# Samples' tile first in the first combine, and the Toeplitz copies of a block issued half by SyncE and half by ScalarE

## The chip, the cores and the metric

The program runs on one core of a Trainium2 chip. The metric is the device time of one launch in microseconds. The engines are TensorE (PE, with PEld for its weight loads), VectorE (DVE), ScalarE (ACT), GpSimd (POOL) and SyncE (SP). SP and ACT also issue DMAs, in program order among their other instructions; a row with SPq or ACTq is such an issue. All data is fp32.

## What is computed

One inference step of a two-layer decoder trunk for 512 prompt tokens and 8 x 8 sample tokens, 576 tokens of width 1024. Layer 0 mixes tokens by sliding-window attention, layer 1 by a diagonal complex state-space layer (S5). After each mixer a mixture of 32 experts with two experts per token is added. Cut to what matters here:

```python
for layer in range(2):
    x += mixer(rmsnorm(x))            # layer 0: attention, layer 1: S5
    x += hier_moe(rmsnorm(x))         # 32 experts, top 2, softmax weights
y = rmsnorm(x)                        # the final norm

# S5: 64 channel groups of 16, each driving a 64-dim complex diagonal state
u = xn.reshape(seq, 64, 16)
bu = einsum('lgc,gpc->lgp', u, bbar)  # complex
h = associative_scan(a_bar, bu)       # over positions
y = real(einsum('lgp,gcp->lgc', h, c)) + d * u
z = gelu(y)
out = (z @ w_a) * sigmoid(z @ w_b)    # the GLU
```

## The kernel before

**Tiles of tokens.** The 576 tokens lie in five tiles of `X`: tiles 0 to 3 are the prompt, 128 tokens each, and tile 4 holds the 64 sample tokens. `XN` holds their normed rows.

**End of the first expert layer.** Sixteen pairs of experts run in order. GpSimd gathers the tokens of a pair and scatters the pair's output rows to `y_scratch` in HBM. SP issues the weight loads (L453 and L459), then the load of a table (L495), the state of the samples (L498), and, once all rows are stored, `rows_back`: five reads of `y_scratch` (L486), tile 0 first. VectorE adds the two rows of each token to `X` (L1476, two instructions a tile, the "combine") and norms the tile before (L737, L740); ScalarE makes the sum of squares and the root between them (L714, L717). Behind `rows_back` SP issues the loads of the first four "blocks" (L376 with `block_scratch`, 1472 KB each), and behind these it waits for each normed tile and copies it from SBUF to SBUF into another layout `AL` (L507), which puts the eight positions of a chunk side by side in one partition: 72 chunks, 64 of the prompt and 8 of the samples. The copy of a prompt tile writes 16 partitions, that of the samples' tile 8.

**The S5 blocks.** The state-space layer runs over `NB` = 8 blocks of 8 channel groups, pipelined by hand: a loop over k on every engine, in which block k enters and block k-2 leaves.

- GpSimd copies the channels of block k out of `AL` (L694, `u_gather`; the first waits for all five copies).
- TensorE: `scan_inputs` transposes the block's weights (L1901) and its inputs (L1909), `taps` makes the taps of a short convolution (L1937), `chunk_sums` the sums of the chunks (L1921), `outputs` the results of block k-2 (L1951, L1955), `mixed_transposed` transposes the results of block k-3 (L1966). L1909 and L1966 write the same PSUM banks, so L1909 of block k waits until the results of block k-4 are copied out.
- ScalarE, in this order in iteration k: copies out the transposed weights (L992) and inputs (L997, L999), GELU of block k-2 (L1005), a copy of the start states (L1009), the taps into `KP` (L1015, four instructions), from k = 2 on the load of block k+2 (L1021), and the transposed results of block k-3 (L1025, two instructions; PE's L1909 waits for them).
- VectorE adds the skip weights to the taps (L1509, which signals `taps_ready`), turns and scans the chunk sums (L1511 to L1528).
- SP waits for `taps_ready` and issues eight copies of 64 KB, SBUF to SBUF (L514), which lay the taps out as a Toeplitz matrix `TT`: one copy for each of the eight shifts, 16 partitions each. `outputs` waits for all eight.

Behind the blocks come the GLU (L2005), the second expert layer and the final norm.

**What sets the order.** Each engine runs the order that is written out in the code; nothing is planned at run time. DMAs issued by SP share one queue, those issued by ACT another. `keep_busy(n, b)` (L1553) is a run of matmuls whose result nobody reads.

## Time and profile before

| what | us |
|---|---|
| median of 3 runs | 944.31 (942.0 to 945.46) |
| profiled execution, its own time | 951.33 |
| span of the profiled execution | 949.6 |
| PE busy | 771.1 (81%) |
| DVE busy | 406.6 (43%) |
| ACT busy | 260.1 (27%) |
| POOL busy | 151.9 (16%) |

Times in the views are microseconds from the start of the span. In a row of the chain of waits the first number is the start, the second the time, and behind them stands what held the chain: an engine with tile and line, a DMA, or an engine's queue. In a row of the timeline the same two numbers are followed by engine, line, operation, output and inputs, and, in brackets, how long the engine had been idle and what ended that. Averages over the span hide the stages: from 482 to 528 PE is nearly idle, and the chain of waits runs through DVE and a DMA there.

### The profile page before, as it was taken

Reading aid. Unit: us, or ns where it says so; the run is one execution under the profiler, and the core shown is the slowest. Engines: PE = TensorE matmul, PEld = TensorE weight load, DVE = VectorE, ACT = ScalarE, POOL = GpSimd, SP = SyncE. Lnnn points to the kernel's source line nnn. Section 1 sums busy time; section 2 is a strip of 40 time slices with the busy share of each in tenths; the row PEclk is TensorE's granted clock in tenths of the full one; section 3 lists DMA queues with packets and bytes.
Section 4 is the critical chain, followed back from the end, with each engine's and each line's share of the span. In section 5 each row is a group of like instructions: output and inputs, shape, how many; then the busy total and the mean of one; then the engine's idle time right before and its main releaser. Section 6 shows DMA issues by size and latency. Waiting matters only on the chain.

```text
span 949.6 us, 12702 instructions
## 1 busy us (share of the span) xinstructions
PE 771.1 (81%) x4843; PEld 480.9 (51%) x4843; DVE 406.6 (43%) x1001; ACT 260.1 (27%) x554; POOL 151.9 (16%) x233
## 2 busy tenths in 40 slices
PE   4999977998999889996810579899999989997840
PEld 3444446777545775554500457644345487554520
DVE  3478686766678441211145556500112162121118
ACT  6020035534121102321131345320014312232113
POOL 1010003000978012332000201000000002322110
PEclk9999996969999789999965789999999979999785
DMA  9461153000633988999779368690041194999946
GB/s 344 135 212 75 50 180 144 2 1 4 212 138 118 335 335 310 409 411 407 304 260 323 46 169 196 136 385 1 17 161 45 68 396 162 408 409 410 402 149 233
DMA packets 74806, 201.81 MB, mean 213 GB/s; under 512 B 14809, under 2 KB 29529, under 8 KB 73689
## 3 DMA queue, kind: packets, MB, share of 16 engines
q1 hardware_dynamic: 57784, 161.77, 47.2%
q0 software_dynamic: 9696, 19.75, 6.0%
q10 hardware_dynamic: 7264, 19.46, 5.6%
q8 instruction: 40, 0.66, 0.3%
q14 instruction: 22, 0.17, 0.1%
HBM read 171.64 MB, written 39.39 MB: 222 GB/s over the span
## 4 chain that ended last, share of the span: by engine, by line
PE 57%; DMA 14%; DVE 11%; SPq 7%; ACT 6%; issue 3%; POOL 0%; PEldq 0%; DVEq 0%; POOLq 0%; PEld 0%; ACTq 0%
PE PSUM L2005 13%; PE PSUM L1598 8%; PE PSUM L1813 8%; PE PSUM L1757 7%; SPq L453 4%; DMA XNT<-in_moe_w_up 4%; PE PSUM L1833 3%; DMA RING<-in_attn_w_qkv 3%; DMA PH<-in_moe_w_up 2%; DVE X L1476 2%; PE PSUM L1801 2%; DMA RING<-XNT 2%; PE PSUM L1688 2%; PE PSUM L1955 2%; PE PSUM L1951 2%
## 5 line engine op out<-in xcount | busy, mean ns | idle before, releaser
L1598 PE MATMUL PSUM<-RING,XNT 128*128 128x512 f32 (+2 forms) x256 | 94.3, 567 | 3.0 <-DMA RING<-in_attn_w_qkv 2.3
L638 POOL DMA_INDIRECT PH<-xn_scratch,PH x32 | 32.6, 1020 | 354.3 <-DVEq L1421 245.6
L2005 PE MATMUL PSUM<-PH,XNT 128*128 128x512 f32 (+1 forms) x220 | 88.1, 593 | 0.3 <-PE PSUM L2005 0.3
L1813 PE MATMUL PSUM<-RING,PH 128*64 128x256 f32 x384 | 75.8, 412 | 13.1 <-DMA PH<-in_moe_w_up 6.6
L1813 PE MATMUL PSUM<-PH 128*64 128x256 f32 x384 | 68.6, 412 | 8.7 <-DMA RING<-in_moe_w_up 5.9
L1452 DVE TENSOR_TENSOR PH<-PH,PSUM 128x128 f32<-128x128 f32 x32 | 9.3, 289 | 145.8 <-ACT PH L943 145.8
L1598 PEld LDWEIGHTS PSUM<-RING,XNT 128*128 128x128 f32 (+1 forms) x256 | 40.3, 177 | 52.4 <-issue 47.7
L1757 PE MATMUL PSUM<-RING,PH 128*128 128x512 f32 (+1 forms) x160 | 62.6, 593 | 0.0
L1813 PEld LDWEIGHTS PSUM<-RING,PH 128*64 128x64 f32 x384 | 44.7, 149 | 34.3 <-issue 18.8
L2005 PEld LDWEIGHTS PSUM<-PH,XNT 128*128 128x128 f32 (+1 forms) x220 | 36.3, 179 | 47.6 <-issue 47.5
L1537 DVE TENSOR_TENSOR PH<-PSUM,PH 128x512 f32<-128x512 f32 (+1 forms) x10 | 6.9, 691 | 115.4 <-ACT PH L1047 115.4
L1813 PEld LDWEIGHTS PSUM<-PH 128*64 128x64 f32 x384 | 40.5, 149 | 28.2 <-issue 13.1
L714 ACT ACTIVATE XNT<-X 128x1024 f32<-128x1024 f32 (+1 forms) x25 | 26.4, 1054 | 103.1 <-DVE X L1334 52.9
L938 ACT ACTIVATE PH<-PSUM 128x1024 f32<-128x1024 f32 x32 | 32.8, 1026 | 67.6 <-PE PSUM L1801 67.6
L647 POOL DMA_INDIRECT y_scratch<-PH x32 | 32.0, 1002 | 91.2 <-DVE PH L1447 89.8
L2005 PE MATMUL PSUM<-RING,XNT 128*128 128x512 f32 (+1 forms) x100 | 43.2, 610 | 1.3 <-ACT XNT L1025 1.3
L1447 DVE COPY PH<-PSUM 128x512 f32<-128x512 f32 x32 | 22.2, 692 | 49.6 <-PE PSUM L1833 25.8
L1757 PEld LDWEIGHTS PSUM<-RING,PH 128*128 128x128 f32 (+1 forms) x160 | 26.3, 179 | 33.2 <-issue 33.2
L943 ACT ACTIVATE PH<-PSUM 128x128 f32<-128x128 f32 x32 | 8.9, 278 | 123.8 <-PE PSUM L1813 123.8
L1555 PE MATMUL PSUM<-ONES,IDENT 128*128 128x128 f32 x296 | 41.0, 308 | 0.2
L1555 PEld LDWEIGHTS PSUM<-ONES,IDENT 128*128 128x128 f32 x296 | 40.3, 223 | 0.5 <-PEq L312 0.5
L1801 PE MATMUL PSUM<-IDENT,PH 128*128 128x128 f32 x256 | 37.4, 290 | 2.2 <-DMA PH<-xn_scratch,PH 2.2
(378 smaller groups left out, 1387.9 us busy)
## 6 DMA issues: line engine op xcount, KB each, us to landing
RING<-in_moe_w_gate SPq DMA_DIRECT2D x24, 512.0 KB
RING<-in_moe_w_up SPq DMA_DIRECT2D x24, 512.0 KB
PH<-in_moe_w_gate SPq DMA_DIRECT2D x24, 512.0 KB
PH<-in_moe_w_up SPq DMA_DIRECT2D x24, 512.0 KB
RING<-in_moe_w_down SPq DMA_DIRECT2D x24, 512.0 KB
PH<-in_moe_w_down SPq DMA_DIRECT2D x24, 512.0 KB
XNT<-in_moe_w_gate SPq DMA_DIRECT2D x16, 512.0 KB
XNT<-in_moe_w_up SPq DMA_DIRECT2D x16, 512.0 KB
```

Of the source, the lines that this page charges most:

```text
L453: sp.dma_start(r[:, w * D:(w + 1) * D].rearrange("p (c f) -> p c f", c=KC), src[layer, e].rearrange("(p c) f -> p c f", p=P)).then_inc(S(f ...
L638: pool.indirect_dma_start(out=XG[:, i % 2, :], out_offset=None, in_=xn_d[layer], in_offset=bass.IndirectOffsetOnAxis(ap=IDX[:, i:i + 1], a ...
L647: pool.indirect_dma_start(out=y_d[layer], out_offset=bass.IndirectOffsetOnAxis(ap=IDXS[:, i:i + 1], axis=0), in_=YB[:, i % 2, :], in_offse ...
L714: nc.scalar.activation(XN[0:r, t, :], X[0:r, t, :], ACT.Square, accum_out=SS[0:r, n, t:t + 1]).then_inc(S("squares"), 1)
L938: nc.scalar.activation(XGT[:, i % 2, :, :], bank(0, 2).rearrange("p b (c t) -> p (b c) t", c=4), ACT.Copy).then_inc(S("xgt_ready"), 1)
L1555: te.matmul(PSUM[:, b, 0:P], IDENT[:, :], ONES[:, :], start=True, stop=True)
L1598: last = te.matmul(PSUM[lo:hi, b0 + col // 512, col % 512:col % 512 + n], XT[:, c, t * P:t * P + r], RING[:, c // 2, (c % 2) * QKV + col:( ...
L1757: last = te.matmul(PSUM[p0:p0 + r, 4 + 2 * (t % 2) + n, :], OT[:, c, t * P:t * P + r], slot(SLOT[q])[:, (c % 3) * D + n * 512:(c % 3) * D ...
L1801: last = te.transpose(PSUM[:, c // 4, (c % 4) * P:(c % 4 + 1) * P], xg[:, c, :], IDENT[:, :])
L1813: last = te.matmul(PSUM[m * 64:(m + 1) * 64, 2 + i % 2, 0:2 * FF], XGT[:, i % 2, c, m * 64:(m + 1) * 64], gu[:, :, c, :], start=(c == 0), ...
L1833: last = te.matmul(PSUM[m * 64:(m + 1) * 64, 4 + 2 * b + n, :], HID[:, b, m, :], r[:, 2 * D + n * 512:2 * D + (n + 1) * 512], start=True, ...
L2005: last = te.matmul(PSUM[p0:p0 + r, 2 * (i % 2) + w, :], XT[:, c, t * P:t * P + r], slot(SLOT[q])[:, (2 * (c % 3) + w) * 512:(2 * (c % 3) + ...
```

## The change

Six edits, all between the end of the first expert layer and the end of the S5 blocks:

1. `rows_back(0)`, the combine and the norm of that place go over the tiles in the order 4, 0, 1, 2, 3 (`TILES`, `tiles`, `place`); so do the copies into `AL`.
2. The loads of blocks 0 and 1 are issued by SP right behind the last expert weights; those of blocks 2 and 3 behind the copies into `AL`.
3. SP issues the first four of the eight Toeplitz copies of a block, ACT the other four, behind its taps (L1015) and ahead of its copy of the transposed results (L1025).
4. ACT issues the load of block 4 in iteration 3 behind L999, not at the end of iteration 2. Blocks 5 to 7 stay where they were.
5. PE runs 16 matmuls of `keep_busy` when all five tiles are combined, ahead of the barrier that ends the stage.
6. PE runs 10 more behind the transposed weights of block 0.

```diff
+        TILES = {2: (4, 0, 1, 2, 3)}
...
             def rows_back(layer):
                 sp.wait_ge(S("all_stored"), layer + 1)
-                for t in range(NT):
+                for t in tiles(2 + 2 * layer):
...
             experts(0)
+            for k in (0, 1):
+                block_in(k)
             sp.wait_ge(S("ring_free"), Q_M0 + 28)
...
             rows_back(0)
-            for k in range(4):
-                ring_load(Q_SSM + k, [(slot(SLOT[Q_SSM + k])[:, 0:BLK_F], blk_d[k])])
-            for t in range(NT):
-                sp.wait_ge(S("xn_done"), 2 * NT + t + 1)
+            for t in tiles(2):
+                sp.wait_ge(S("xn_done"), place(2, t) + 1)
                 rows = AL[t:PCH:4, :, :] if t < 4 else AL[PCH:NCH, :, :]
                 sp.dma_start(rows, XN[0:ROWS[t], t, :]).then_inc(S("al_in"), 16)
+            for k in (2, 3):
+                block_in(k)
...
-                for sh in range(L):
+                for sh in range(L // 2):
                     sp.dma_start(TT[...], KP[...]).then_inc(S(f"toeplitz{k % 3}"), 16)
...
+                    if k == 3:
+                        block_in(4)
...
                     ins.then_inc(S("kp_ready"), 1)
-                    if 4 <= k + 2 < NB:
+                    if 5 <= k + 2 < NB:
+                        block_in(k + 2)
+                if k < NB:
+                    act.wait_ge(S("taps_ready"), k + 1)
+                    if k >= 3:
+                        act.wait_ge(S("y_ssm"), k - 2)
+                    for sh in range(L // 2, L):
+                        act.dma_start(TT[...], KP[...]).then_inc(S(f"toeplitz{k % 3}"), 16)
...
                     last.then_inc(S("st_transposed"), 1)
+                    pe.wait_ge(S("x_updated"), 2 * NT)
+                    keep_busy(16, 7)
                 end_phase(pe, ph)
...
                 last.then_inc(S("w_transposed"), 1)
+                if k == 0:
+                    keep_busy(10, 7)
```

On SP, between the last expert weights and the Toeplitz copies of block 1. Before (`in_moe_w_down` are the last expert weights, `input_scratch` the table, `RING<-XNT` the copies into `AL`, `PH<-PH` the Toeplitz copies), with the empty overflow branch between the states and `y_scratch` left out:

```order
L459 DMA XNT<-in_moe_w_down 128x1024 [waits expert_out] x2
L495 DMA PH<-input_scratch 128x1600 [waits ring_free]
...
L486 DMA XNT<-y_scratch 128x2x1024 x2
L486 DMA PH<-y_scratch 64x2x1024
L376 DMA RING<-block_scratch 128x2944 [waits ring_free]
L376 DMA PH<-block_scratch 128x2944 [waits ring_free] x3
L507 DMA RING<-XNT 16x8x1024 [waits xn_done] x4
L507 DMA RING<-XNT 8x8x1024 [waits xn_done]
L514 DMA PH<-PH 16x8x128 [waits taps_ready]
L514 DMA PH<-PH 16x8x128 x7
```

On SP, the same stretch in the changed kernel:

```order
L468 DMA XNT<-in_moe_w_down 128x1024 [waits expert_out] x2
L385 DMA RING<-block_scratch 128x2944 [waits ring_free]
L385 DMA PH<-block_scratch 128x2944 [waits ring_free]
L509 DMA PH<-input_scratch 128x1600 [waits ring_free]
...
L495 DMA PH<-y_scratch 64x2x1024 [waits all_stored]
L495 DMA PH<-y_scratch 128x2x1024 x2
L495 DMA XNT<-y_scratch 128x2x1024 x2
L519 DMA RING<-XNT 8x8x1024 [waits xn_done]
L519 DMA RING<-XNT 16x8x1024 [waits xn_done] x4
L385 DMA PH<-block_scratch 128x2944 [waits ring_free] x2
L528 DMA PH<-PH 16x8x128 [waits taps_ready]
L528 DMA PH<-PH 16x8x128 x3
```

No block load stands between the reads of `y_scratch` and the copies into `AL` any more; two went ahead of the reads and two behind the copies, and four of the Toeplitz copies left the queue.

On ACT, iteration 4 of the block loop, from GELU to the transposed weights of the next iteration. Before (`RING<-PSUM` is GELU, `PH<-XNT` the start states, `PH<-PSUM 16x2x128` the taps, `XNT<-PSUM` the transposed results, `RING<-PSUM 128x1024` the weights):

```order
L1005 ACTIVATE RING<-PSUM 72x4x8x16 [waits u_gathered,y_ssm]
L1005 ACTIVATE RING<-PSUM 72x4x8x16
L1009 ACTIVATE PH<-XNT 128x8x8
L1015 ACTIVATE PH<-PSUM 16x2x128 [waits toeplitz2,taps]
L1015 ACTIVATE PH<-PSUM 16x2x128 x3
L1021 DMA PH<-block_scratch 128x2944 [waits ring_free]
L1025 ACTIVATE XNT<-PSUM 128x8x64 [waits z_transposed]
L1025 ACTIVATE XNT<-PSUM 128x8x8
L992 ACTIVATE RING<-PSUM 128x1024 [waits g_done,w_transposed]
```

On ACT, the same iteration in the changed kernel:

```order
L1026 ACTIVATE RING<-PSUM 72x4x8x16 [waits u_gathered,y_ssm]
L1026 ACTIVATE RING<-PSUM 72x4x8x16
L1030 ACTIVATE PH<-XNT 128x8x8
L1036 ACTIVATE PH<-PSUM 16x2x128 [waits toeplitz2,taps]
L1036 ACTIVATE PH<-PSUM 16x2x128 x3
L1004 DMA PH<-block_scratch 128x2944 [waits ring_free]
L1046 DMA PH<-PH 16x8x128 [waits y_ssm,taps_ready]
L1046 DMA PH<-PH 16x8x128 x3
L1052 ACTIVATE XNT<-PSUM 128x8x64 [waits z_transposed]
L1052 ACTIVATE XNT<-PSUM 128x8x8
L1011 ACTIVATE RING<-PSUM 128x1024 [waits g_done,w_transposed]
```

A wait on VectorE's `taps_ready` and four DMA issues now stand between the taps and the copy of the transposed results.

## Rows read from the trace of the kernel before

**Rows 1.** Page, part 4: shares of the chain that ended last, by engine.

```profile
PE 57%; DMA 14%; DVE 11%; SPq 7%; ACT 6%; issue 3%; POOL 0%; PEldq 0%; DVEq 0%; POOLq 0%; PEld 0%; ACTq 0%
```

**Rows 2.** Chain of waits from the rows' return to the first block: start, time, what.

```profile
482.27 5.25 DMA PH<-y_scratch
...
507.11 1.29 DVE XNT L740
508.41 19.49 DMA RING<-XNT
...
528.02 1.04 POOL PH L694
```

**Rows 3.** Timeline of SP's issues in the same stretch: block loads, copies into AL.

```profile
485.86 1.41 SPq L376 DMA_DIRECT2D PH<-block_scratch  x3
494.55 14.60 SPq L507 DMA_DIRECT2D RING<-XNT  x5
```

**Rows 4.** Windows: span, busy PE, PEld, DVE, ACT, POOL, clock, DMA share, GB/s.

```profile
460.00:485.00 25.00, 15.29 (x114) 8.86 (x114) 3.24 (x7) 4.46 (x7) 3.92 (x4) 0.94 0.56 203
485.00:512.00 27.00, 1.97 (x8) 1.57 (x8) 22.75 (x27) 9.52 (x17) 0.00 (x0) 0.50 1.02 385
512.00:522.00 10.00, 0.00 (x0) 0.00 (x0) 1.86 (x5) 0.00 (x0) 0.00 (x0) 0.50 1.01 200
522.00:526.00 4.00, 0.00 (x0) 0.00 (x0) 0.00 (x0) 0.00 (x0) 0.00 (x0) 0.50 0.50 83
535.00:540.00 5.00, 3.38 (x80) 2.93 (x80) 4.86 (x9) 3.58 (x9) 1.59 (x2) 1.00 0.70 88
```

**Rows 5.** DMA issues by tile, with KB each and median us to landing.

```profile
out<-XNT SPq DMA_DIRECT2D x4, 512.0 KB, 2.6
```

**Rows 6.** Chain of waits, one period of the block loop (iteration 6).

```profile
582.06 0.59 ACT RING L1005
...
584.38 1.25 ACT XNT L1025 x2
...
585.77 0.69 PE PSUM L1909 x8
...
590.44 0.61 PE PSUM L1955 x8
```

**Rows 7.** Timeline of DVE: the taps' addition in iteration 5, and what it waited for.

```profile
574.95 0.29 DVE L1509 TENSOR_TENSOR PH<-PH 16x128 f32<-16x128 f32 x1 [2.02 <-ACT PH L1015]
```

**Rows 8.** Source views, ns min/median/max of one issue: Toeplitz copies on SP, ACT's issues.

```profile
L514 SPq DMA_DIRECT2D PH<-PH x64: 585/601/1811, 533.4 to 608.3; - x64
L1037 ACTq DMA_DIRECT2D out<-PH x4: 442/449/454, 623.3 to 625.2; - x4
L873 ACTq DMA_DIRECT2D out<-PH x1: 1038/1038/1038, 132.3 to 132.3; - x1
```

**Rows 9.** Timeline of PE: the outputs of blocks 1 and 7 begin.

```profile
555.57 1.13 PE L1951 MATMUL PSUM<-PH,XNT 128*72 128x128 f32 x4 [5.06 <-DMA PH<-PH]
...
611.65 1.13 PE L1951 MATMUL PSUM<-PH,XNT 128*72 128x128 f32 x4 [3.16 <-DMA PH<-PH]
```

**Rows 10.** Chain of waits: the outputs of blocks 1, 5 and 7 end.

```profile
561.91 0.61 PE PSUM L1955 x8
...
599.93 0.61 PE PSUM L1955 x8
...
617.32 0.61 PE PSUM L1955 x8
```

**Rows 11.** Windows before and after the outputs of block 7 begin, columns as in rows 4.

```profile
608.50:611.60 3.10, 0.00 (x0) 0.00 (x0) 1.10 (x4) 1.24 (x3) 0.00 (x0) 1.00 0.80 114
611.70:614.50 2.80, 2.80 (x16) 2.17 (x16) 0.00 (x0) 0.00 (x0) 0.00 (x0) 0.50 1.01 351
```

**Rows 12.** Timeline: keep_busy of 20 matmuls ahead of the experts, ACT's table load for GELU.

```profile
324.42 6.56 PE L1555 MATMUL PSUM<-ONES,IDENT 128*128 128x128 f32 x40
...
540.75 1.28 ACT L1005 ACT_TABLE_LOAD   x1
```

More of the change, by code:

```diff
@@ L359, in router_load, with tiles, place @@
             queue.dma_start(BR[:, 4:36], b_re_r[layer:layer + 1, :].to_broadcast([P, 32])).then_inc(S("router_in"), 16)
+        TILES = {2: (4, 0, 1, 2, 3)}
+        def tiles(n):
+            return TILES.get(n, range(NT))
+        def place(n, t):
+            return NT * n + list(tiles(n)).index(t)
         block = ctx.enter_context(nc.Block())
@@ L492, in _, with block_in @@
             sp.dma_start(in_d[:, 2 * GP * CH:], PWRQ.rearrange("p r k g -> p (r k g)")).then_inc(S("bb_out"), 16)
+            def block_in(k):
+                ring_load(Q_SSM + k, [(slot(SLOT[Q_SSM + k])[:, 0:BLK_F], blk_d[k])])
             experts(0)
+            for k in (0, 1):
+                block_in(k)
             sp.wait_ge(S("ring_free"), Q_M0 + 28)
@@ L711, in norm_act @@
             else:
-                act.wait_ge(S("x_updated"), NT * (n - 1) + t + 1)
+                act.wait_ge(S("x_updated"), place(n, t) - NT + 1)
             r = ROWS[t]
@@ L734, in norm_dve @@
         def norm_dve(dve, ch, n, t):
-            dve.wait_ge(S("roots"), NT * n + t + 1)
+            dve.wait_ge(S("roots"), place(n, t) + 1)
             r = ROWS[t]
             ch(nc.vector.reciprocal(RSTD[0:r, n, t:t + 1], RSTD[0:r, n, t:t + 1]))
-            if t == 0:
+            if t == tiles(n)[0]:
                 dve.wait_ge(S("gamma_in"), 16 * (n + 1))
@@ L980, in moe @@
                                          ).then_inc(S("hs_in"), 1)
-                for t in range(NT):
+                for t in tiles(2 + 2 * layer):
                     norm_act(act, 2 + 2 * layer, t)
@@ L985, in _, with block_in @@
             moe(0, 4)
+            def block_in(k):
+                q = Q_SSM + k
+                act.wait_ge(S("ring_free"), freed(q))
+                act.dma_start(slot(SLOT[q])[:, 0:BLK_F], blk_d[k]).then_inc(S(f"ring_full{SLOT[q]}"), 16)
             for k in range(NB + 3):
@@ L1017, in _ @@
                     ins.then_inc(S("kp_ready"), 1)
-                    if 4 <= k + 2 < NB:
-                        q = Q_SSM + k + 2
-                        act.wait_ge(S("ring_free"), freed(q))
-                        act.dma_start(slot(SLOT[q])[:, 0:BLK_F], blk_d[k + 2]).then_inc(S(f"ring_full{SLOT[q]}"), 16)
+                    if 5 <= k + 2 < NB:
[5 more added lines that the diff above has]
+                    for sh in range(L // 2, L):
+                        act.dma_start(TT[CH * sh:CH * sh + CH, k % 3].rearrange("p w g n -> p (w g) n"),
+                                      KP[k % 2][:, :, :, 112 - CH * sh:240 - CH * sh].rearrange("p w g n -> p (w g) n")
+                                      ).then_inc(S(f"toeplitz{k % 3}"), 16)
                 if k >= 3:
@@ L1470, in moe @@
                                            ).then_inc(S("ov_dve"), 1)
-                for t in range(NT):
+                norm = 2 + 2 * layer
+                for j, t in enumerate(tiles(norm)):
                     r = ROWS[t]
@@ L1477, in moe @@
                                                 in1=X[0:r, t, :], op0=ALU.mult, op1=ALU.add).then_inc(S("yg_used"), 1)
-                        dve.wait_ge(S("yg_used"), (layer * NT + t) * 2 + k + 1)
+                        dve.wait_ge(S("yg_used"), (layer * NT + j) * 2 + k + 1)
                     dve.sem_inc(S("x_updated"), 1)
-                    if t:
-                        norm_dve(dve, ch, 2 + 2 * layer, t - 1)
-                norm_dve(dve, ch, 2 + 2 * layer, NT - 1)
+                    if j:
+                        norm_dve(dve, ch, norm, tiles(norm)[j - 1])
+                norm_dve(dve, ch, norm, tiles(norm)[-1])
                 end_phase(dve, ph)
```

2 lines of the change are left out of this document (1 added, 1 removed).

## The prediction

> **What bounds the kernel now.** I read the page first, then the chain of waits. The chain is 57% PE and 14% DMA [rows 1], but the change touches only the stretch from the last experts to the GLU, so the page's shares decide nothing; that stretch has to be read by itself. There the chain runs through three things, and the reader should see them one after the other.
>
> First, the return of the rows: the read of tile 0 lands 5.25 us after its issue, at 487.5, VectorE then combines and norms five tiles until 508.4, and the last copy into `AL` lands 19.49 us later, at 527.9, when GpSimd begins block 0 [rows 2]. The windows say why that copy takes so long: the DMA engines are full at 385 GB/s from 485 to 512, then full at only 200 GB/s until 522, then half busy at 83 GB/s until 526 [rows 4]. The first stretch is the reads and the four block loads, 6.0 MB, which SP issued by 487.3, ahead of the first copy at 494.6 [rows 3]; the second is the copies, which queue behind them.
>
> Second, the loop over the blocks. From iteration 3 on it has a period of 9.5 us, one closed ring: GELU at 582.06, the other ACT work up to the transposed results at 584.38, PE's L1909 at 585.77, outputs until 591.05, GELU again [rows 6]. VectorE and SP hang on it with time to spare.
>
> Third, two waits of PE for Toeplitz copies, 5.06 us ahead of the outputs of block 1 and 3.16 us ahead of those of block 7 [rows 9].
>
> **The change part by part.** Sums are made against the profiled execution's own 951.33 us, which stands 7.0 us above the median of the runs; a difference is carried over as it is.
>
> *The return of the rows.* The samples' read is 512 KB, not 1024 KB, and is issued first. At the 385 GB/s of rows 4 half of 1 MB is 1.4 us; I take 1.2. The combine's chain of 20.9 us (487.5 to 508.4) has the same instructions, so it ends at 507.2. The last copy is now that of tile 3, 512 KB, with a queue that holds no block load ahead of it: the copies are 2.4 MB and at 200 GB/s one takes 2.6 us, under the 4.1 us that a tile takes on VectorE, so nothing piles up. A lone 512 KB store lands 2.6 us after its issue [rows 5], of which 1.3 are its bytes at 385 GB/s; 1.3 + 2.6 is 3.9 us, and with a tail as from 522 to 526 it would be 8. I take 4.4. So `AL` is complete at 511.6 instead of 527.9: **-16.3 us** (bounds -12.7 and -16.8).
>
> By the Trainium skill ("DMA: Bandwidth & Descriptors", "Why a DMA increments its semaphore by 16 and not by 1") a copy whose slower side has 8 partitions runs on 8 of the 16 engines, which would explain the half busy tail as the samples' copy; going first it would leave the end, and the term is -16.3. If the tail belonged to any such copy, the term would be -12.7; the rows alone don't tell the two apart.
>
> *Blocks 0 and 1 earlier.* 3.0 MB, 7.8 us at 385 GB/s. They are issued at about 458 behind the last weights, and from 460 to 485 the DMA engines are 44% idle [rows 4], 11 us. So they fit, at no cost; without that cover they would push the reads of `y_scratch` back by up to their own 7.8 us. Blocks 2 and 3 are issued behind the copies, at about 508, and land by 520, when the first Toeplitz copies are issued; block 2 is needed at about 522. No cost.
>
> *keep_busy.* 20 matmuls took 6.56 us from a cold start [rows 12], so 16 take some 5 us. They begin when the last tile is combined, at about 504, and end at 509, 1 us past VectorE; but GpSimd now waits until 511.6. VectorE's 5.4 us of set-up begin 1 us later and are needed at 517. The 10 further ones fit before 512.7. No cost; the first block starts warm, worth up to 1 us, which I leave out.
>
> *The start of the loop.* Split between two queues, with no block load beside them (block 4 is now issued later, past the copies of block 1), the Toeplitz copies of block 1 no longer hold PE: 5.06 us of wait and 2.3 us of slow clock behind it (6.95 us for those outputs [rows 9, 10] against 4.7 in rows 6) go away. Against that, ACT waits in iteration 1 until VectorE is done with block 0 and issues its four copies there; its 1.28 us table load, which lay in idle time [rows 12], comes out ahead of GELU. **-6.1 us.**
>
> *The period.* In iterations 3 to 7 ACT waits for `taps_ready` before it copies out the transposed results, and PE's L1909 waits for these; whatever ACT does there lengthens the ring. VectorE is already waiting for the taps [rows 7], so the wait is its 0.29 us and two signals, 0.4 us. The issues are not in the trace of before on ACT: their nearest row is the same copy on SP, 0.60 us [rows 8], 0.64 from one start to the next, 2.56 for four. ACT's other issues run from 0.45 to 1.04 [rows 8]; 0.60 is the same transfer, so I take it. 2.95 us more per period; between the outputs of block 1 and those of block 5 lie four periods (562.5 to 600.5 now [rows 10]): **+11.8 us** (bounds +8.8 and +18.2).
>
> *The clock.* PE reaches L1909 about when ACT is done now (ACT ends at 585.63, L1909 begins at 585.77 [rows 6]), so the 2.95 us become idle time of PE, once in each period. Ahead of the outputs of block 7 it idled 3.16 us, and came back at the lower of the clock's two levels, 1.2 GHz: granted clock 0.50 for 2.8 us [rows 9, 11]. Half speed for 2.8 to 3 us loses 1.4 to 1.5 us, in each of four periods: **+6.0 us** (bounds 0 and +9, the upper from the 4.5 us that the outputs of block 1 stayed slow).
>
> *The end of the loop.* From the outputs of block 5 to the end of those of block 7 it is 17.4 us now [rows 10]. Eight issues on SP are 5.1 us and the last lands 3.35 later; with four on each queue the issues take 2.6 us, and then the bytes bind: 512 KB at 88 GB/s and a share of 0.70 [rows 4] are 4.2 us of full DMA. So the copies land some 2 us earlier, PE's wait falls under 1.5 us, and with it 1.4 us of slow clock: **-3.1 us**.
>
> The Trainium skill ("DMA: Bandwidth & Descriptors", "Issuing engines are not separate DMA queues") speaks against the split: both queues feed the same 16 engines, and only the issue time is saved. By that alone this term would be -2.6, and by the rows -3.1.
>
> The sum: -16.3 - 6.1 + 11.8 + 6.0 - 3.1 = -7.7 us. Behind the loop (GLU, second experts) everything starts from the loop's end, so it moves along: 951.3 becomes 943.6 in a profile, and the median 944.3 becomes **936.6 us**.
>
> **The rivals.**
> - *A cheap ring.* PE's clock holds through the idle stretches, or ACT issues in 0.45 us as it does its small stores [rows 8], so that the idle stretch is 2.2 us. For it: 2.95 us is less than the 3.16 of rows 9. Against: by little. Without the 6.0 us of slow clock it gives -13.7; with 0.45 us an issue, 3 us less in four periods, -10.7 with the slow clock and -16.7 without: 927 to 934.
> - *A dear ring.* The clock stays down 4.5 us as it did from 555.5, or two queues slow each other's issues to 0.8 us. Then -1 to -4.5: 940 to 943.
> - *Slower than before.* ACT's issue of a copy costs what its store at L873 cost, 1.04 us. The period grows by 4.6 us, four times, with the slow clock behind it: 18.4 + 9 against 25.5 of gains and some 0.7 for the table load and iteration 2: +2 to +5, 946 to 949. With the slow clock at its upper bound it decides from 0.93 us an issue. Against it: L873 was issued right behind another store; no copy of the Toeplitz shape took over 0.6 us in the median.
> - *Not what it says.* Blocks 0 and 1 delay the last scatters or the reads, since the idle 44% is uneven between the 16 engines. The reads start 3 to 5 us later and the gain falls to 3 to 5 us: 939 to 941.
>
> **How the numbers follow.** The forecast 0.46; the cheap ring 0.26; the dear ring 0.15; late reads 0.07; slower 0.06. The range 927 to 943.5 leaves out the slow rival and the far ends of the cheap and the dear ring. A measurement of this kernel can tell about 0.5%, 4.7 us. Faster by more is the forecast, the cheap ring and a little of the late reads, 0.74; within it lie the rest of these, the dear ring and the near end of the slow rival, 0.22; slower, its far end, 0.04.
>
> **What would show each step.** The last copy into `AL` lands at about 512 and takes under 5 us. No DMA wait of PE ahead of the outputs of block 1. In iterations 4 to 7 four DMA issues on ACT between the taps and the transposed results, a period of 12.4 us with a granted clock of 1.00 or about 14 with 0.50 behind the idle stretch. The forecast is wrong if the copy still ends after 516, if the period stays at 9.5, or if it passes 15.

## The result, and the profile after

The changed kernel takes 964.28 us in the median (962.1 to 969.93), the kernel before 944.29 us (942.0 to 945.46) on the same chip: a ratio of 1.023, interval 1.019 to 1.027. It is slower by 20 us, where 936.6 was forecast, a gain of 8. The two profiled executions differ by less, 949.6 and 960.3 us of span: the one of before lay 7 us above its median, that of after 2 us below its own, and the code ahead of the changed stretch, the same in both, happened to take 5 us less in the latter.

Cut at five events that both traces have, the stretch reads as follows (each event's start, taken from the timelines of GpSimd and ACT; the GELU events are ACT's first GELU of a block).

| stage | before, us | after, us | difference | forecast |
|---|---|---|---|---|
| scatter of pair 12 to the issue of the reads of `y_scratch` | 21.6 | 26.9 | +5.4 | 0 |
| issue of the reads to GpSimd's first copy of block 0 | 45.8 | 32.1 | -13.7 | -16.3 |
| that copy to the GELU of block 1 | 34.5 | 30.5 | -4.0 | -6.1 |
| GELU of block 1 to GELU of block 5 | 38.0 | 66.4 | +28.4 | +17.8 |
| GELU of block 5 to GELU of block 7 | 17.4 | 17.5 | +0.1 | -3.1 |

Everything behind that moves along, as was forecast: 331.7 us from the GELU of block 7 to the end before, 331.4 after.

The first two rows of the table, from the chain of waits. Before, the last scatter landed in 3.21 us:

```profile
478.75 3.21 DMA y_scratch<-PH
```

In the chain of after (start, time, what) two scatters of the last pairs land 10.20 and 6.36 us after they start; the read of the first tile takes 5.51 us, against 5.25 in [rows 2], though it is the samples' half tile now; VectorE is done with its five tiles at 508.8. There the chain passes over to the engines' meeting at the end of the phase.

```profile
463.94 10.20 DMA y_scratch<-PH
...
475.77 6.36 DMA y_scratch<-PH
...
482.43 5.51 DMA PH<-y_scratch
...
507.52 1.28 DVE XNT L754
508.80 0.05 DVEq L312
508.85 2.98 issue
```

And SP's timeline there (start, time, line, issue): the loads of blocks 0 and 1 stand behind the last expert's weights, ahead of those scatters, and blocks 2 and 3 behind the copies to `AL`, where [rows 3] had the block loads ahead of them. GpSimd's first copy begins at 514.50, 5.7 us after the last norm.

```profile
452.90 2.90 SPq L385 DMA_DIRECT2D RING<-block_scratch  x1
455.84 1.06 SPq L385 DMA_DIRECT2D PH<-block_scratch  x1
...
494.94 14.42 SPq L519 DMA_DIRECT2D RING<-XNT  x5
509.40 2.08 SPq L385 DMA_DIRECT2D PH<-block_scratch  x2
```

GpSimd's copy is not what the chain goes through, though. The "issue" of 2.98 us behind 508.85 is VectorE waiting for the end of the phase, which TensorE's 16 matmuls of `keep_busy` hold until 511.76 (timelines of PE and DVE):

```profile
505.83 5.93 PE L1583 MATMUL PSUM<-ONES,IDENT 128*128 128x128 f32 x32 [21.60 <-DVEq L1507]
511.86 0.07 DVE L1515 MEMSET PH<- 128x16 f32 x1 [3.06 <-PEq L312]
```

VectorE's set-up of the loop then takes 7.9 us, to 519.77, and the first Toeplitz issue follows at 519.79. Before, the same set-up took 5.4 us. Three of its operations, 0.42 to 0.59 us each before, take 1.02 to 1.34 here, beside GpSimd's copies (514.50 to 518.21), which lay behind the set-up before. One of them, before and after:

```profile
512.25 0.42 DVE L1069 TENSOR_TENSOR PH<-PH,XNT 128x256 f32<-128x256 f32 x1
```

```profile
516.29 1.02 DVE L1096 TENSOR_TENSOR PH<-PH,XNT 128x256 f32<-128x256 f32 x1
```

The fourth row is where the time went. One period of the loop in the chain of after, to be laid beside [rows 6]:

```profile
578.30 0.58 ACT RING L1026
...
580.21 0.38 ACT PH L1036
...
580.69 0.30 DVE PH L1537
...
581.01 0.60 ACTq L1046
...
581.63 0.87 ACTq L1046
...
582.54 1.70 ACTq L1046
...
584.26 1.84 ACTq L1046
...
587.03 0.33 ACT XNT L1052
...
587.50 1.19 PE PSUM L1941 x8
588.69 0.85 PE PSUM L1983 x4
589.54 1.06 PE PSUM L1987 x8
...
594.28 0.61 PE PSUM L1987 x8
```

The reader is to see two things. ACT's four issues (L1046) stand on the ring, between VectorE's addition to the taps and ACT's copy of the transposed results (L1052), as forecast; but the first alone takes 0.60 us, the others 0.87, 1.70 and 1.84, together 5.09 and not 2.56. And TensorE, which waits all that time, comes back at half speed: its first groups of eight matmuls take 1.06 us, at the end of the block 0.61. From ACT's copy of the transposed results to GELU it needs 7.5 us against 5.4. The period is 17.1 us instead of 9.5: 5.5 us are the issues and the wait for VectorE, 2.1 the slow matmuls.

The first period, from block 1 to block 2, is as long (16.1 us) for another reason as well: block 4's load is issued behind ACT's four copies, at 543.47, and TensorE waits for it (timeline of PE, with what it waited for):

```profile
552.22 1.97 PE L1931 MATMUL PSUM<-IDENT,RING 128*128 128x128 f32 x8 [4.87 <-DMA RING<-block_scratch]
```

### The profile page after: what moved, and what is told of

Read it like the earlier page. It is cut to its first block, busy times and chain, and to the rows that moved or that the text cites. A ratio compares the mean times of both kernels' runs of the same rounds, so it can differ in the third digit from the quotient of the medians.

```text
span 960.3 us, 12811 instructions
## 1 busy us (share of the span) xinstructions
PE 775.3 (81%) x4895; PEld 486.6 (51%) x4895; DVE 405.5 (42%) x1001; ACT 259.5 (27%) x554; POOL 151.9 (16%) x233
## 4 chain that ended last, share of the span: by engine, by line
PE 57%; DMA 12%; DVE 11%; SPq 8%; ACT 6%; issue 3%; ACTq 3%; PEldq 0%; DVEq 0%; POOL 0%; PEld 0%; POOLq 0%
PE PSUM L2037 13%; PE PSUM L1626 8%; PE PSUM L1841 7%; PE PSUM L1785 6%; SPq L462 5%; PE PSUM L1861 3%; DMA RING<-in_attn_w_qkv 3%; ACTq L1046 3%; SPq L468 2%; PE PSUM L1583 2%; PE PSUM L1829 2%; DVE X L1504 2%; DMA y_scratch<-PH 2%; DMA XNT<-in_moe_w_up 2%; DMA RING<-in_moe_w_up 2%
## 5 line engine op out<-in xcount | busy, mean ns | idle before, releaser
L652 POOL DMA_INDIRECT PH<-xn_scratch,PH x32 | 32.5, 1016 | 369.2 <-DVEq L1448 263.1
L1841 PE MATMUL PSUM<-RING,PH 128*64 128x256 f32 x384 | 73.3, 404 | 13.1 <-DMA PH<-in_moe_w_up 6.7
L1841 PE MATMUL PSUM<-PH 128*64 128x256 f32 x384 | 66.0, 404 | 10.7 <-DMA RING<-in_moe_w_up 6.1
L1583 PE MATMUL PSUM<-ONES,IDENT 128*128 128x128 f32 x348 | 50.5, 316 | 21.8 <-DVEq L1507 21.6
L1583 PEld LDWEIGHTS PSUM<-ONES,IDENT 128*128 128x128 f32 x348 | 49.4, 231 | 22.2 <-DVEq L1507 21.7
L1841 PEld LDWEIGHTS PSUM<-PH 128*64 128x64 f32 x384 | 39.6, 147 | 30.5 <-issue 16.3
L728 ACT ACTIVATE XNT<-X 128x1024 f32<-128x1024 f32 (+1 forms) x25 | 26.4, 1054 | 101.0 <-DVE X L1361 52.5
L952 ACT ACTIVATE PH<-PSUM 128x1024 f32<-128x1024 f32 x32 | 32.8, 1025 | 67.0 <-PE PSUM L1829 67.0
L1474 DVE COPY PH<-PSUM 128x512 f32<-128x512 f32 x32 | 22.1, 692 | 51.7 <-PE PSUM L1861 24.8
```

The lines of the kernel that those rows point to most:

```text
L652: pool.indirect_dma_start(out=XG[:, i % 2, :], out_offset=None, in_=xn_d[layer], in_offset=bass.IndirectOffsetOnAxis(ap=IDX[:, i:i + 1], a ...
L952: nc.scalar.activation(XGT[:, i % 2, :, :], bank(0, 2).rearrange("p b (c t) -> p (b c) t", c=4), ACT.Copy).then_inc(S("xgt_ready"), 1)
L1583: te.matmul(PSUM[:, b, 0:P], IDENT[:, :], ONES[:, :], start=True, stop=True)
L1841: last = te.matmul(PSUM[m * 64:(m + 1) * 64, 2 + i % 2, 0:2 * FF], XGT[:, i % 2, c, m * 64:(m + 1) * 64], gu[:, :, c, :], start=(c == 0), ...
```

## The experiments

Fifteen runs were made, of fourteen kernels (`e19_sp_all_blk4` is `e10_sp_all_blk4_old` again); each ratio is to the kernel before on the same chip, with its 95% interval. Line numbers differ a little from kernel to kernel. Each run has one profile. The two of the same kernel, `e10_sp_all_blk4_old` and `e19_sp_all_blk4`, differ by 2.3 us in the first stage of the table above and by 3.7 us from GpSimd's first copy to the GELU of block 7, while the periods of the ring agree within 0.1 us; so differences of 2 or 3 us between single stages outside the ring prove little.

### Which part costs: the split alone, and all but the split

`e1_sp_all` is the changed kernel with SP issuing all copies again:

```
-                for sh in range(L // 2):
+                for sh in range(L):
...
-                if k < NB:
-                    act.wait_ge(S("taps_ready"), k + 1)
...
-                    for sh in range(L // 2, L):
-                        act.dma_start(TT[CH * sh:CH * sh + CH, k % 3]...
```

> The changed kernel with one part undone: the sync engine issues all eight Toeplitz copies of a block, ACT none. Theory (the copies in ACT's own order are what costs): the period of the loop over blocks falls from 16.6 us back to 9.5 to 10 us, four periods give back about 26 us, and the end of the loop takes back about 2 us: 936 to 941 us, since the rows still come back early. Rival (the loop is slow for another reason that came with the change: it begins earlier, so that block 4's load and the scattered rows fall into it): the periods stay above 13 us and the time stays at 952 to 964 us.

941.61 us, ratio 0.9977 (0.9946 to 1.0008): the loss of 20 us is gone, and the time lies just above the range of the theory. The periods from block 2 to block 5 are 9.5 us. The first is not, it is 14.9, so that a theory of one cause does not cover it; see block 4 below.

`e2_split_only` is the kernel before with that part and nothing else.

> The kernel before with one part of the change alone: the sync engine issues the first four copies of a block, ACT the other four between its taps and its transposed results; nothing else is moved. Theory (the split alone costs what the loop lost): the four periods go from 9.5 to about 16.6 us, plus 28 us, less about 4 us at the start of the loop, where TensorE waited for block 1's copies: 964 to 970 us. Rival (the loss needs the earlier start of the loop as well): the periods grow by no more than the 4 us that were predicted, and the time is 950 to 957 us.

975.05 us, ratio 1.0315 (1.0264 to 1.0367), 5 us above what was expected. All four periods are 16.8 to 17.6 us, 69.2 us from block 1 to block 5. The split does it by itself, and the rest of the change is worth about nothing without it (-0.2%) and 0.9% beside it (1.023 against 1.0315).

### Why the issues take so long: two engines at once

`e9_act_all` lets ACT issue all eight copies and SP none. In `e4_one_by_one` SP holds its four until ACT has issued its own:

```
             for k in range(NB):
                 sp.wait_ge(S("taps_ready"), k + 1)
...
+                if k >= 3:
+                    sp.wait_ge(S("zt_ready"), k - 2)
```

> The changed kernel with ACT issuing all eight copies of a block and the sync engine none, so that no two engines issue them at once. Theory (two engines that issue at once lengthen each other's issues): eight issues by ACT alone cost 0.6 us each, 4.8 us, which is what four cost now, so the period stays near 16.6 us: 958 to 972 us. Rival (an issue by ACT is slow by itself, about 1.2 us whoever else issues): eight take 9 to 10 us, the periods grow by some 5 us each, and the time is 984 to 1000 us.

> The changed kernel in which the sync engine, from block 3 on, holds its four issues until ACT has issued its own four and copied the transposed results behind them; blocks 0 to 2 are issued as in the changed kernel. Theory (two engines that issue at once lengthen each other's issues): from block 3 on ACT's four issues take 2.4 to 2.6 us instead of 4 to 5, the periods fall by about 2 us each, more if TensorE keeps its clock: 948 to 958 us. Rival (ACT's issues are slow by themselves): they still take 4 to 5 us and the time stays at 961 to 968 us.

`e9_act_all` took 983.07 us (1.0401, 1.0342 to 1.0461), `e4_one_by_one` 960.55 us (1.0167, 1.0117 to 1.0216). The source views give the time of one issue (ns min/median/max). Of the changed kernel, both engines at once:

```profile
L1046 ACTq DMA_DIRECT2D PH<-PH x32: 596/880/1838, 519.8 to 617.3; - x32
...
L528 SPq DMA_DIRECT2D PH<-PH x32: 585/634/1948, 519.8 to 616.8; - x32
```

Of `e9_act_all`, ACT alone:

```profile
L1046 ACTq DMA_DIRECT2D PH<-PH x64: 592/622/1432, 522.7 to 632.4; - x64
```

Of `e4_one_by_one`, one after the other from block 3 on:

```profile
L1048 ACTq DMA_DIRECT2D PH<-PH x32: 592/622/1521, 522.5 to 613.5; - x32
...
L530 SPq DMA_DIRECT2D PH<-PH x32: 585/601/1545, 522.5 to 617.3; - x32
```

In the median an issue by ACT is as cheap as one by SP in [rows 8], 0.62 us, as long as the other engine does not issue too. When both do, the third and fourth of each engine are mostly the slow ones: ACT's four took 5.09 us in the period above and 4.1 to 4.6 in the rounds of blocks 4, 6 and 7, against 2.55 in `e4_one_by_one`. There the periods from block 2 to block 5 fall from 50.4 to 44.1 us, 2.1 us each, which is what the issues lost. Its time is 4 us below the changed kernel's (6 by the ratios), just above the 948 to 958 that the theory expected; the end of the loop, whose last copies now start later, gave 1.7 us back. For `e9_act_all` neither theory had the time right: eight issues by ACT alone cost 5.2 to 6.9 us in the ring, more than the four contended ones, the periods are 17.3 to 18.8 us, and at the end of the loop (26.4 us instead of 17.5) all eight wait their turn in ACT's order.

Two things keep this from being a plain rule. Alone, an engine is not always fast either: the kernel before needs 5.1 us for its eight where no block load runs beside them (blocks 6 and 7), but 6.5 to 6.9 us in blocks 2 to 5, where two or three of the eight take 1.0 to 1.8 us. Counted from the first issue to the end of the last, the split therefore did shorten the issuing, from 6.5 and 6.9 to 4.6 and 5.1 us in blocks 4 and 5 and from 5.1 to 4.1 in blocks 6 and 7; what it did not do is halve it, and it put ACT's share on the ring, where none had been. And in the round of block 3 of the changed kernel both engines issue from the same moment, yet ACT's four take 2.90 us (SP's end at 550.83):

```profile
548.23 2.90 ACTq L1046 DMA_DIRECT2D PH<-PH  x4
```

The same round takes 2.83 to 2.86 us in `e3_behind`, `e11_ring_busy` and `e18_ring_busy20`. In these four kernels the loads of blocks 4 and 5 are issued just ahead of it, at 543.47 and 546.00 here, and fill the DMA engines (416 GB/s from 548.2 to 551.2). With block 4's load earlier the round takes 5.07 us (`e14_blk4_old`) and 4.66 us (`e17_behind_blk4`), as the others do. So issuing at once lengthens the issues, as `e4_one_by_one` shows, but not in every state of the queues; what else it takes was not tested.

The Trainium skill ("Perfetto Trace Analysis", "DMA Instruction — HWDGE (DVE, Sync)") says that the profiled time of such a DMA instruction includes the wait for a descriptor generator, which is locked for exclusive use while it serves one instruction. The slow rounds look like that; the round of block 3, in which two engines needed little more than half of what one needs, does not. The runs show the length of the issues, not the lock.

### Where the issues stand

`e3_behind` only moves the four issues behind ACT's copy of the transposed results:

```
                     ins.then_inc(S("kp_ready"), 1)
+                if k >= 3:
+                    act.wait_ge(S("z_transposed"), k - 2)
...
                 if k < NB:
                     act.wait_ge(S("taps_ready"), k + 1)
...
-                if k >= 3:
-                    act.wait_ge(S("z_transposed"), k - 2)
...
```

> The changed kernel with ACT's four issues moved behind its copy of the transposed results in the same round, so that TensorE no longer waits for them there. Theory (what costs is that the issues stand between ACT's taps and that copy, on the ring of the loop): TensorE's wait shrinks to under 1 us, the clock stays up, and the period falls to 10.5 to 12 us, since ACT then has about 6 us of its own work and 4.5 us of issues in each: 942 to 952 us. Rival (ACT's total of work and issues, or the copies' landing, sets the period wherever they stand): the period stays above 15 us, 958 to 966 us.

943.4 us, ratio 0.9994 (0.9958 to 1.0029), at the good end. The issues are as slow as before (median 0.88 us), and the periods from block 2 on are 9.5 us: better than expected, because ACT's own work and its issues do fit. The first is 16.2 us, with block 4's load; with that load at its old place it is 9.5 too (`e17_behind_blk4`, below). The timeline of that kernel (ACT, ACT's issues and PE; the bracket is PE's wait):

```profile
574.02 1.13 ACT L1044 ACTIVATE XNT<-PSUM 128x512 f32<-128x512 f32 x1
...
574.42 0.60 ACTq L1053 DMA_DIRECT2D PH<-PH  x1
...
575.04 4.08 ACTq L1053 DMA_DIRECT2D PH<-PH  x3
575.41 0.69 PE L1941 MATMUL PSUM<-IDENT,PH 72*128 72x72 f32 x8 [0.20 <-ACT XNT L1044]
```

TensorE waits 0.20 us, and the 4.7 us of issues lie beside its outputs. So it is the place in ACT's order that cost, and the slow issues only set how much.

### How much is TensorE's clock

`e11_ring_busy` and `e18_ring_busy20` add matmuls of the identity by ones to the changed kernel, in the time in which TensorE waits for ACT:

```
+                if k >= 5:
+                    pe.wait_ge(S("z_ready"), k - 2)
+                    keep_busy(20, 7)
```

(`e11_ring_busy`: `k >= 4` and 30.)

> The changed kernel with one addition: in the rounds of blocks 4 to 7 TensorE runs 30 matmuls of the identity by ones (about 4.9 us) while it waits for ACT's copy of the transposed results, that is, while ACT issues its four copies. Theory (part of what the loop lost is TensorE's clock, at its lower level for some 4 us after each such wait): the granted clock stays at 1.00, the outputs of a block take 4.7 instead of 6.2 us, each of four periods falls by about 2 us: 954 to 958 us. Rival (the matmuls themselves hold TensorE, or the clock has little part in it): 961 to 968 us.

> The changed kernel with 20 matmuls of the identity by ones in the rounds of blocks 5 to 7 alone, while TensorE waits for ACT; 30 of them (e11_ring_busy) kept the granted clock at 1.00 but lasted 1.6 us beyond the wait, and in the round of block 4 there was no wait to fill. Theory (of the 7.1 us that a period grew, some 5.3 are ACT's issues and the wait for VectorE ahead of them, some 1.8 TensorE's lower clock behind the wait): three periods fall from 16.8 to 14.5 to 15.2 us, 957 to 961 us. Rival (the clock is not what lengthens the outputs, or has no part in the period): the periods stay at 16 us or more, 963 to 967 us.

`e11_ring_busy` took 969.83 us (1.0268, 1.0201 to 1.0335), slower: its 30 matmuls lasted 6.9 us, 1.2 to 1.7 beyond the copy that TensorE waits for, and in the round of block 4, where TensorE had been waiting for the load and not for ACT, they came on top (first period 23.1 us); the other three periods fall to 15.8 us. `e18_ring_busy20` took 960.08 us (1.0175, 1.0130 to 1.0219), as the theory said. Windows of a stretch (columns as in [rows 4]), first two of the changed kernel, then one of `e18_ring_busy20`:

```profile
580.00:585.00 5.00, 1.21 (x11) 0.86 (x9) 4.18 (x9) 0.57 (x2) 0.00 (x0) 1.00 0.83 305
585.00:590.00 5.00, 2.50 (x18) 2.21 (x20) 2.11 (x6) 2.77 (x5) 0.00 (x0) 0.53 0.65 74
```

```profile
580.00:600.00 20.00, 17.24 (x215) 15.24 (x216) 9.67 (x22) 6.55 (x15) 0.00 (x0) 1.00 0.49 112
```

TensorE is idle for 5.7 us ahead of 587.50, and the 0.53 is the mean of a fall: microsecond by microsecond the granted clock is 0.50 from 586 to 592, the lower of its two levels, 1.2 GHz, and 1.00 again from 593. Kept busy, it stays at 1.00. ACT's issues are no shorter in `e18_ring_busy20` (4.78, 5.45 and 4.12 us). The three periods from block 2 to block 5 fall from 50.4 to 44.1 us: **2.1 us per period are the clock**. What is left of the 16.8 us that a period takes on average is 9.5 + 5.2, and 5.2 us are ACT's issues with the wait ahead of them.

### Block 4's load

`e10_sp_all_blk4_old` is `e1_sp_all` with block 4's load back in the round of block 2; `e14_blk4_old` does the same in the changed kernel.

```
-                    if k == 3:
-                        block_in(4)
...
-                    if 5 <= k + 2 < NB:
+                    if 4 <= k + 2 < NB:
```

> The run in which the sync engine issues all copies (e1_sp_all), with block 4's load back at the place that it has in the kernel before, in the round of block 2 behind the taps instead of in the round of block 3. Theory (in e1_sp_all block 4's load, issued 1.3 us behind the first of block 2's copies, meets them, so that the last of these lands 8.3 us after its issue and TensorE waits 8 us): issued some 3 us earlier it is done earlier, the wait shrinks to 3 to 6 us, and the time is 937 to 940 us. Rival (load and copies need the same engines whatever the order): within 1.5 us of e1_sp_all, 940 to 943 us.

> The changed kernel, its copies still split, with block 4's load back at the place of the kernel before (the round of block 2, behind the taps). With all copies on the sync engine this place was worth 8 us (e10_sp_all_blk4_old against e1_sp_all). Theory (behind ACT's issues the first period is as long as the others anyway, so the load's wait is mostly covered): the first period goes from 16.1 to 14 to 16 us, 960 to 964 us. Rival (the load's lateness adds to the rest in full): the first period falls to 11 us or less and the time is 954 to 959 us.

`e10_sp_all_blk4_old`: 933.54 us (0.9884, 0.9824 to 0.9944), faster than the kernel before; the same kernel again as `e19_sp_all_blk4`: 936.35 us (0.992, 0.9882 to 0.9957). The first time is below both expectations, the second just above its own: the wait did not shrink, it went, and the first period is 9.5 us instead of 14.9. In the chain of `e1_sp_all` the last of block 2's copies is late:

```profile
538.04 0.58 SPq L528
...
542.91 8.29 DMA PH<-PH
551.24 1.13 PE PSUM L1975 x4
```

and the load was issued among them at 539.38, in the timeline of `e10_sp_all_blk4_old` 2.2 us ahead of them:

```profile
536.50 0.33 ACTq L1004 DMA_DIRECT2D RING<-block_scratch  x1
...
538.71 15.82 SPq L528 DMA_DIRECT2D PH<-PH  x16
```

With the copies split the place is worth nothing: `e14_blk4_old` took 967.42 us (1.025, 1.0161 to 1.0339), its first period 17.9 us, longer than either theory had it: ACT's issues and the slow clock fill it anyway.

### Blocks 0 and 1, and keep_busy

Three kernels vary where the first blocks are loaded. `e7_sp_all_later` (from `e1_sp_all`) has 0 and 1 behind the reads; `e13_block0_reads` (from `e10_sp_all_blk4_old`) has 0 behind the reads and 1 behind the copies to `AL`; `e16_block1_late` (from the same) leaves 0 behind the last expert and loads 1 behind the copies to `AL`. `e12_sp_all_no_busy16` is `e1_sp_all` without `keep_busy(16, 7)`.

```
             experts(0)
-            for k in (0, 1):
-                block_in(k)
...
             rows_back(0)
+            block_in(0)
...
-            for k in (2, 3):
+            for k in (1, 2, 3):
                 block_in(k)
```

> The run in which the sync engine issues all copies (e1_sp_all), with a second part of the change undone: blocks 0 and 1 are loaded right behind the reads of y_scratch, ahead of the reads' rows going to AL, and no longer behind the last expert's weights. Theory (these two loads stand ahead of the last pairs' scattered rows and hold them up): from the scatter of pair 12 to the reads' issue it takes 21 to 22.5 us again instead of 27, and of these 5 us at most 2 are lost again where the two blocks meet the copies to AL: 936 to 940 us. Rival (the last scatters are long for another reason, or the loads only move the wait): 940 to 945 us, with that stage still at 26 us or the five copies to AL ending as much later.

> The fastest run so far (e10_sp_all_blk4_old: all copies on the sync engine, block 4's load at its old place), with block 0 loaded behind the reads of y_scratch and block 1 behind the copies to AL, with 2 and 3. Theory (blocks 0 and 1 cost 5 us ahead of the last scatters, or 4.5 us ahead of the copies to AL, wherever both are loaded; block 1 is not needed until a few us into the loop): from the scatter of pair 12 to the reads' issue it takes 21 to 22 us, from there to the first copy of GpSimd 32 to 34 us, and the time is 927 to 932 us. Rival (block 1 then lands late and the loop waits for it, or block 0 alone delays the copies to AL by as much): 932 to 938 us.

> As e10_sp_all_blk4_old, with block 0 left behind the last expert's weights and only block 1 loaded behind the copies to AL, with 2 and 3. Theory (the last scatters wait for bytes that stand ahead of them): half the bytes, half the delay, 24 to 25 us from the scatter of pair 12 to the reads' issue instead of 27, nothing lost at AL: 929 to 933 us. Rival (block 1 then lands late and the loop waits for it): 933 to 938 us.

> The run in which the sync engine issues all copies (e1_sp_all), without the sixteen matmuls that the change adds to keep TensorE busy ahead of the end of the phase. Theory (these matmuls hold the end of the phase, and with it VectorE's set-up of the loop, by some 3 us): VectorE's first set-up operation follows its last norm by less than 1 us instead of 3, and the time is 938 to 940 us. Rival (without them TensorE's clock is at its lower level when the loop begins, and what is won there is lost): 941 to 945 us.

| kernel | median, us | ratio | scatter of pair 12 to reads | reads to GpSimd's first copy |
|---|---|---|---|---|
| `e1_sp_all` | 941.61 | 0.9977 | 26.9 | 32.1 |
| `e7_sp_all_later` | 940.57 | 0.9951 (0.9918 to 0.9985) | 21.6 | 36.7 |
| `e19_sp_all_blk4` | 936.35 | 0.9920 | 26.7 | 32.8 |
| `e13_block0_reads` | 932.87 | 0.9865 (0.9799 to 0.9932) | 20.4 | 32.5 |
| `e16_block1_late` | 936.11 | 0.9916 (0.9875 to 0.9957) | 23.7 | 32.1 |

The last scatter in the chain of `e7_sp_all_later` lands in 3.21 us again instead of 6.36, but its last copy to `AL` needs 9.65:

```profile
480.36 3.21 DMA y_scratch<-PH
...
510.75 9.65 DMA RING<-XNT
```

So two block loads cost 5 us wherever they stand ahead of something that is waited for; in `e7_sp_all_later` the wait was only moved, as the rival said. The first stage repeats well: in all profiles with both loads ahead of the scatters it is 26.6 to 27.0 us, but for 29.0 in `e10_sp_all_blk4_old`, and without them 20.4 to 22.1. With one of the two, `e16_block1_late`, it is 23.7, a little less than half the delay, as expected, but the time is that of `e19_sp_all_blk4` and in the rival's range. `e13_block0_reads` pays neither, 5 to 6 us by these two stages, but its loop begins 2 us later behind GpSimd's first copy, where the last of block 0's copies lands 4.40 us after its issue instead of 2.79 in `e1_sp_all`; its time is the best here, at the foot of the rival's range, and not apart from `e10_sp_all_blk4_old` by the intervals. `e12_sp_all_no_busy16` took 943.21 us (0.9983, 0.9945 to 1.0021): VectorE's set-up does begin 3 us earlier there, right behind its last norm, but `AL`'s last copy (5.52 us) then sets the pace: from the last norm to the first Toeplitz issue it takes 10.3 us, against 10.9 in `e1_sp_all`, and no difference shows in the time.

### Does the split save anything out of the ring

`e17_behind_blk4` is `e3_behind` with block 4's load at its old place, and differs from `e19_sp_all_blk4`, run beside it, in the split and in what that makes of ACT's order.

> The changed kernel with two edits: ACT's four issues behind its copy of the transposed results (as in e3_behind) and block 4's load at the place of the kernel before. It differs from e19_sp_all_blk4, run beside it, in nothing but who issues the copies and what ACT's order makes of that. Theory (the split shortens nothing, since the two engines' issues slow each other, and out of the ring it costs nothing): within 3 us of e19_sp_all_blk4, 932 to 938 us. Rival (out of the ring the split does save the 2 to 3 us at either end of the loop that were forecast): 927 to 931 us, faster than e19_sp_all_blk4 by 3 us or more.

> The same kernel as e10_sp_all_blk4_old (all copies on the sync engine, block 4's load at its old place), again, as the measure for e17_behind_blk4 on the same chip: 931 to 936 us.

`e17_behind_blk4`: 941.0 us (0.9964, 0.9936 to 0.9992), 4.6 us above `e19_sp_all_blk4`, which neither expected. In the profiles the loop does not differ by so much: from GpSimd's first copy to the GELU of block 7 it takes 86.7 us in the one and 85.8 in the other (82.1 in `e10_sp_all_blk4_old`), and the rest of their distance lies ahead of the reads, in code that is the same. What made it so stays open. That the split brings the landing no earlier is plain at the end of the loop, in the chain of `e17_behind_blk4` and of `e19_sp_all_blk4`, the copies of block 7:

```profile
595.12 5.27 DMA PH<-PH
600.43 1.13 PE PSUM L1981 x4
```

```profile
585.99 0.58 SPq L528
...
590.47 3.23 DMA PH<-PH
593.75 1.13 PE PSUM L1973 x4
```

On two engines the last issue comes earlier but lands 5.27 us later instead of 3.23; from GELU of block 5 to that of block 7 it is 18.0 us in the one and 18.2 in the other.

## Why the prediction was wrong, point by point

- **What bounds the kernel.** The reading of the kernel before holds: the return of the rows, the ring of 9.5 us and the waits for copies. It was right that whatever ACT does ahead of L1052 lengthens the ring.
- **The period: the step that failed.** "0.60 is the same transfer, so I take it": the same transfer costs 0.62 us on ACT, but not while SP issues its own four at the same moment. The term was +11.8 us, 2.95 us in a period, and measured 5.2 us in the mean of the three periods from block 2 to block 5, some +21 over four (the first period has block 4's load in it as well). That lies above even its upper bound, +18.2, which came from a store at 1.04 us. The rival of the dear ring had the mechanism, two queues slowing each other's issues, and priced it at 0.8 us; in the period shown the issues behind the first took 0.87 to 1.84. The price left out a sign in its own row: [rows 8] has 0.60 in the median but 1.81 at most, and the eight issues of one block took up to 6.9 us there, not 5.1. The slower rival had nearly the size, 1.04 us an issue, with no mechanism for it. A row that shows an issue alone, read by its median, is no price for one beside another.
- **The clock.** +6.0 us forecast; 2.1 us in a period, some +8 us in four. The mechanism was right; the idle stretch was longer than thought (5.7 us, not 2.95), and the clock stayed down for some 4.5 us of matmuls behind it (587.5 to 592 in the period shown), the case of the upper bound, not 2.8 to 3.
- **The return of the rows.** -16.3 forecast, -13.7 measured, inside its bounds. The samples' half tile saved nothing of the read's 5.3 us (1.2 was taken), and GpSimd began 5.7 us after the last norm, where the last copy was to be complete after 4.4.
- **Blocks 0 and 1 earlier, "no cost".** Wrong: +5.4 us. The idle 44% of the DMA engines is an average over 25 us; what the chain waits for there is the scatter of one pair's rows, and it lands late when 3 MB are put ahead of it. The rival of the late reads had this, 3 to 5 us, but not what came on top; its reason, an uneven load of the 16 engines, was not looked at.
- **The start of the loop.** -6.1 forecast, -4.0 measured. PE's wait ahead of the outputs of block 1 did go. The 2 us that are missing are no more than two profiles of one kernel differ by in this stage (26.9 and 29.7 us, `e10_sp_all_blk4_old` and `e19_sp_all_blk4`); in the chain of after they lie with VectorE's set-up, 7.9 us and not 5.4, and with ACT's four issues for block 0, 4.5 us ahead of its copy of block 1's weights. What was not seen is that block 4's load, moved past that point, lands among block 2's copies: it cost 5.4 us in the first period when the copies were not split, and was covered by ACT's issues when they were.
- **keep_busy, no cost:** the number holds, the reason does not. The 16 matmuls ended at 511.76 and not at 509, and VectorE's set-up, which waits for them, began 3 us late and was on the chain, where GpSimd's wait was to cover it. Without them another wait takes its place and no time is won (`e12_sp_all_no_busy16`).
- **The end of the loop.** -3.1 forecast, +0.1 measured: eight issues took 4.1 us on two engines there against 5.1 on one, not 2.6, and the bytes landed no earlier: 7.9 us from the first issue to the last landing in the changed kernel, 7.8 in the kernel before, 7.7 in `e19_sp_all_blk4`. The sentence of the Trainium skill ("DMA: Bandwidth & Descriptors", "Issuing engines are not separate DMA queues") that only issue time is saved would have given -2.6; here 1.0 us of issue time was saved, and none of it reached the landing.

By the rows of the first table the terms add up to +16 us instead of -7.7; the other 4 of the 20 us between the medians are not placed: each kernel has one profile, and the stretch ahead alone differs by 5.2 us between the two. What beats both kernels, by about 1%, is the change without its split and with block 4's load left where it was: 933.5 and 936.4 us in two runs, 932.9 with block 0 loaded behind the reads as well and block 1 behind the copies to `AL`.

## What to carry to other kernels

Before a DMA issue is handed to a second engine, look at what stands behind it in that engine's order: a few issues in front of an instruction on a closed ring cost their full length in every period, and nothing in the period one place further back (9.5 us in `e3_behind`). Price an issue that runs beside others by a row that shows them together, and look at the longest time in a row beside its median. A load that is moved into "idle" DMA time has to be checked against the small transfer that is waited for there, not against the mean share.

## What the runs showed of the hardware

- An issue of a 64 KB copy by ACT took 0.62 us in the median when ACT issued alone (`e9_act_all`) and 0.88 when SP issued beside it; in the period shown 0.60 for the first and 0.87 to 1.84 for those behind it. In blocks 4 to 7 eight took 4.1 to 5.1 us on two engines and 5.1 to 6.9 on SP alone (changed kernel and kernel before), but 2.90 on two in the round of block 3, behind two block loads.
- TensorE's granted clock was 0.50 when work came back after 5.7 us without matmuls, and stayed at 1.00 when 20 small ones filled 4.6 us of them.
- Three operations of VectorE's set-up, on 128x256, took 1.02 to 1.34 us beside GpSimd's copies (changed kernel) and 0.42 to 0.59 us without them (kernel before).
- A 1.5 MB load issued 2.2 us ahead of eight 64 KB copies held nobody up, the same load 1.3 us behind the first of them made the last copy land 8.3 us after its issue.
- The stretch ahead of the changed one is not the same length in each execution: GpSimd's scatter of pair 12 started between 455.1 and 462.3 us in the profiles of these kernels, with the same code ahead. Stages are compared here from event to event for that reason.
